# Two narrow projections made one unit: the low-rank gate and the forget gate of a hybrid decoder layer

## The reference

```
h = x + 0.5 * post1(swiglu1(pre1(x)))              # gate, up, down
p = preM(h) @ w_in                                 # 1024 -> 512 | 784 | 768 | 772 columns
ya = conformer_conv(p[A]); yb = gla(p[B]); yc = short_conv(p[C]); yd = fox(p[D])
h = h + postM(concat(ya, yb, yc, yd) @ w_out)
h = h + 0.5 * post2(swiglu2(pre2(h)))

gla:  q, k, v, g, a_lr = split(p[B])               # a_lr has 16 columns
      log_a = log_sigmoid(a_lr @ w_a2 + b_a) / 16  # decay of every state row, summed in chunks of 64
fox:  q, k, v = p[D][:768]; logf = log_sigmoid(p[D][768:] + b_f)   # 4 columns, one for a head
      scores = q k / 8 + cumsum(logf)[query] - cumsum(logf)[key]; softmax; @ v
      (sample positions: the same against 256 cached rows per sequence)
```

## Time and profile before

| | |
|---|---|
| median of 3 runs | 1095.44 us (1094.72 to 1095.91) |
| profiled execution, its own time | 1094.53 us |
| its span | 1092.7 us |
| mean granted TensorE clock | 0.993 of full |
| PE busy | 1064.1 us (97%), 8956 matmuls |
| DVE busy | 705.6 us (65%) |
| ACT busy | 550.6 us (50%) |
| POOL busy | 274.5 us (25%) |
| phase "in" of layer 0 | from about 211 to 325 us of the span; layer 1 from about 748 to 861 us |

### The profile page before, as it was taken

How to read it: one execution, slowest core, us unless ns; L and a number is a source line. 1 busy time by engine, 2 the same in 40 slices (tenths; PEclk the granted TensorE clock), 3 DMA queues, 4 the chain that set the end, 5 groups by cost and what they waited for, 6 DMA issues and landing times. The chain is left out here.

```text
span 1092.7 us, 24133 instructions
## 1 busy us (share of the span) xinstructions
PE 1064.1 (97%) x8956; PEld 1028.8 (94%) x8956; DVE 705.6 (65%) x1045; ACT 550.6 (50%) x887; POOL 274.5 (25%) x340
## 2 busy tenths in 40 slices
PE   6999999989999999999999999999899999999997
PEld 5999999988879999999999999998888899999997
DVE  5666644589995766654476665436999776666443
ACT  6544454554357644454474445446534675444542
POOL 3222221304504322220132223012053042222200
PEclk9999999999999999999999999999999999999999
DMA  7666677342726566656646666763426257656561
GB/s 269 207 186 180 179 222 232 98 155 79 232 78 196 155 193 180 184 166 187 188 127 203 180 180 188 232 186 117 139 79 209 79 190 217 180 179 176 178 181 53
DMA packets 63747, 186.92 MB, mean 171 GB/s; under 512 B 9515, under 2 KB 19763, under 8 KB 63539
## 3 DMA queue, kind: packets, MB, share of 16 engines
q1 hardware_dynamic: 63666, 185.81, 56.2%
HBM read 182.40 MB, written 3.38 MB: 170 GB/s over the span
## 5 line engine op out<-in xcount | busy, mean ns | idle before, releaser
L313 DVE TENSOR_TENSOR w_lo<-raw,w_hi 128x1024 fp32r<-128x1024 f32 (+1 forms) x316 | 411.1, 1306 | 332.0 <-ACT w_hi L303 331.8
L303 ACT ACTIVATE w_hi<-raw 128x1024 fp32r<-128x1024 f32 x336 | 342.9, 1026 | 283.0 <-PE ub L345 188.4
L343 PE MATMUL ub<-hg_hi,w_hi 128*128 128x264 f32 x960 | 278.7, 290 | 6.3 <-DVE proj L1315 6.3
L344 PE MATMUL ub<-hg_lo,w_hi 128*128 128x264 f32 x960 | 274.9, 286 | 0.0
L345 PE MATMUL ub<-hg_hi,w_lo 128*128 128x264 f32 x960 | 274.6, 286 | 0.0
L343 PE MATMUL ub<-act_hi,w_hi 128*128 128x264 f32 x704 | 200.5, 285 | 0.0
L345 PE MATMUL ub<-act_hi,w_lo 128*128 128x264 f32 x704 | 200.0, 284 | 0.0
L344 PE MATMUL ub<-act_lo,w_hi 128*128 128x264 f32 x704 | 199.1, 283 | 0.0
L343 PE MATMUL quad<-hg_hi,w_hi 128*128 128x264 f32 x688 | 196.4, 285 | 0.0
L344 PE MATMUL quad<-hg_lo,w_hi 128*128 128x264 f32 x688 | 194.9, 283 | 0.0
L345 PE MATMUL quad<-hg_hi,w_lo 128*128 128x264 f32 x688 | 194.8, 283 | 0.0
(11 more groups left out here) (252 smaller groups left out, 1314.4 us busy)
## 6 DMA issues: line engine op xcount, KB each, us to landing
raw<-in_w_gu SPq DMA_DIRECT2D x176, 512.0 KB, 4.1
raw<-in_w_dn SPq DMA_DIRECT2D x64, 512.0 KB, 4.1
raw<-in_w_in SPq DMA_DIRECT2D x44, 512.0 KB, 3.8
raw<-in_w_dn SPq DMA_DIRECT2D x32, 384.0 KB, 3.7
raw<-in_w_out SPq DMA_DIRECT2D x16, 512.0 KB, 3.7
pages<-in_cache_k SPq DMA_DIRECT2D x32, 128.0 KB, 3.3
pages<-in_cache_v SPq DMA_DIRECT2D x32, 128.0 KB, 3.1
con<-in_con SPq DMA_DIRECT2D x1, 1448.0 KB
```

The costliest lines, as they stand in the source:

```text
L303: eng.activation(w_hi[:, slot, 0:w], raw[:, slot, 0:w], ACT.Copy).then_inc(*sig("hi_ready", reps))
L313: eng.tensor_tensor(w_lo[:, slot, 0:w], raw[:, slot, 0:w], w_hi[:, slot, 0:w].bitcast(F32), ALU.subtract)\
L343: eng.matmul(out, a_hi, x_hi[:, k0 + k, :], start=(first and k == 0), stop=False)
L344: eng.matmul(out, a_hi, x_lo[:, k0 + k, :], start=False, stop=False)
```

## The change

The 16 columns of the low-rank gate and the 4 columns of the forget gate become one unit of 36 columns: columns 0 to 15 and 32 to 35, with zeros between. Phase "in" has 23 units then; the 24th place of the ring stays empty, so that later units keep their slots and the semaphore counts (the last unit counts twice). Every unit behind the first has a number one lower. `mix(l, n)` runs at step n-1 on ACT, DVE and SP, and behind unit n-1 on PE, so it stands at the same unit by content. Beyond that:

- PE's small matmul of the GLA gate goes from n=3 to n=4 (with the new numbers still behind unit 3); ACT's softplus of it and the scaling of q go from n=4 to n=3, so to step 2. DVE's part stays at n=4, so at step 3.
- The forget gate's softplus goes from n=2 to n=7 on ACT, its DVE chain from n=3 to n=9. It works on partitions 32 to 35 now.
- `decode_scores` goes from n=15 to n=14 on PE, ahead of the unit it stood behind, and ACT copies `qd` before `qm`.

The engines' instruction lists show three places. In them `w_hi` is the rounding of a unit, `h_sq<-mb` the start of the GLA gate's softplus, `ln_t` the forget gate's softplus and `z_t` and `y_sq` the DVE chains of the GLA gate and of the forget gate.

The diff, cut to its core:

```diff
-ALR, FG, BQ, BK, AG, BG, AV, BV, DQ, DKK, DVV, CC, CX, CB = 0, 1, 2, 3, 4, 6, 8, 10, 12, 14, 16, 18, 19, 22
-IN_WIDTH = [16, 4] + [P] * 22
+ALR, FG, BQ, BK, AG, BG, AV, BV, DQ, DKK, DVV, CC, CX, CB = 0, 0, 1, 2, 3, 5, 7, 9, 11, 13, 15, 17, 18, 21
+IN_UNITS = 23
+FG_ROWS = slice(32, 36)
+IN_WIDTH = [FG_ROWS.stop] + [P] * (IN_UNITS - 1)
...
-POOLED = tuple(range(14, 24))
+POOLED = tuple(range(13, 23))
...
+        def no_unit(phase, idx):
+            return phase == "in" and idx == IN_UNITS
+        def counted(phase, idx):
+            return 2 if phase == "in" and idx == IN_UNITS - 1 else 1
+        def empty_turns(layer, phase, slot):
+            if slot != IN_UNITS % RING:
+                return 0
+            return layer + (phase in ("out", "gu1", "dn1"))
...
             def mix(l, n):                                   # PE
-                if n == 3:
+                if n == 4:
                     after(l, proj=1)
                     pe.matmul(mb[2][:, 0:NT], par[0:16, ...], proj[0:16, ALR, :], ...).then_inc(*sig("b_z"))
...
-                if n == 15:
+                if n == 14:
                     decode_scores(l, 0)
                     decode_scores(l, 1)
+                if n == 15:
                     gla_outputs(l)
...
-                for n in range(GROUP, 24):
+                for n in range(GROUP, IN_UNITS):
...
-                    mix(l, n)
+                    mix(l, n + 1)
...
             def mix(l, n):                                   # ACT
-                if n == 4:
+                if n == 3:
                     after(l, b_z=1)
                     softplus(l, soft[:, :], mb[2][:, 0:NT], ...)
-                if n == 2:
-                    after(l, proj=2)
-                    softplus(l, lft[:, :], proj[0:H, FG, :], ...)
-                if n == 4:
-                    after(l, proj=3)
+                if n == 7:
+                    after(l, proj=1)
+                    softplus(l, lft[:, :], proj[FG_ROWS, FG, :], ...)
+                if n == 3:
+                    after(l, proj=2)
                     act.activation(proj[:, BQ, :], proj[:, BQ, :], ACT.Copy, scale=DK ** -0.5)
...
             def mix(l, n):                                   # DVE
-                if n == 3:
-                    after(l, d_sp=3, proj=2)
+                if n == 9:
+                    after(l, d_sp=3, proj=1)
                     log_sigmoid(l, lf[:, :], proj[FG_ROWS, FG, :], ..., "d_lf")
...
-                    mix(l, s)
+                    mix(l, s + 1)
```

More of the change, by code:

```diff
@@ L326, in fourth_unit @@
             first = PHASES[phase][0]
-            return dict(index=3, phase=phase, layer=l, width=COLS, slot=3, number=l * UNITS + first + 3, turn=l * (UNITS // RING) + first // RING)
+            return dict(index=3, phase=phase, layer=l, width=COLS, slot=3, number=l * UNITS + first + 3,
+                        turn=l * (UNITS // RING) + first // RING - empty_turns(l, phase, 3))
         def final(l, q):
@@ L335, in first_unit, with multiply_unit @@
             return dict(index=s, phase="gu0", layer=0, weights=ins["w_gu0"], row=s, width=COLS, slot=s, number=s, turn=0)
-        def multiply_unit(eng, out, slot, x_hi, x_lo, tiles, k0, first, last, reps, ready=None):
+        def multiply_unit(eng, out, slot, x_hi, x_lo, tiles, k0, first, last, reps, ready=None, count=1):
             for k in range(tiles):
@@ L622, in fox_scores @@
             def fox_scores(l, h):
-                after(l, d_qm=2, d_cf=2, proj=16, b_rs=2, b_og=3)
+                after(l, d_qm=2, d_cf=2, proj=15, b_rs=2, b_og=3)
                 for out, q0, n in ((fox_bank[h][:, 0:P], 0, P), (fox_bank[h][:, P:3 * P], P, TP)):
                     pe.matmul(out, qm[:, h, q0:q0 + P], proj[:, DKK + h // 2, 0:n], start=True, stop=False)
-                    mm = pe.matmul(out, const("sel", H * P, H)[:, h * P:(h + 1) * P], cf[:, 0:n], start=False, stop=True)
+                    mm = pe.matmul(out, sel[:, h * P:(h + 1) * P], cf[:, 0:n], start=False, stop=True)
                 mm.then_inc(*sig("d_sc"))
@@ L845, in rows, with softplus @@
                 return slice(CH * i, CH * (i + 1))
-            def softplus(l, out, x, bias, name):
+            def softplus(l, out, x, bias, one, name):
                 act.activation(out, x, ACT.Abs, bias=bias).then_inc(*sig(name))
@@ L852, in softplus @@
                 after(l, **{name: 2})
-                act.activation(out, out, ACT.Ln, bias=biases[0:out.shape[0], 2:3]).then_inc(*sig(name))
+                act.activation(out, out, ACT.Ln, bias=one).then_inc(*sig(name))
             def level_decays(l, i):
@@ L893, in mix @@
                 if n == 14:
-                    after(l, proj=14, d_qz=1)
-                    for i in range(2):
-                        act.activation(qm[rows(i), i::2, :], proj[rows(i), DQ:DQ + 2, :], ACT.Copy).then_inc(*sig("d_qm"))
+                    after(l, proj=13, d_qz=1)
                     for j in range(2):
@@ L902, in mix @@
                                .then_inc(*sig("d_qd"))
+                    for i in range(2):
+                        act.activation(qm[rows(i), i::2, :], proj[rows(i), DQ:DQ + 2, :], ACT.Copy).then_inc(*sig("d_qm"))
                 if n == 16:
@@ L1086, in level_keys @@
             def level_keys(l, i):
-                after(l, b_E=i, proj=4, b_qs=1)
+                after(l, b_E=i, proj=3, b_qs=1)
                 if i >= 3:
@@ L1148, in mix @@
                 if n == 12:
-                    after(l, proj=12)
+                    after(l, proj=11)
                     for j in range(2):
@@ L1178, in mix @@
                 if n == 16:
-                    after(l, proj=16)
+                    after(l, proj=15)
                     dve.wait_ge(zeroed, 1)
```

79 lines of the change are left out of this document (41 added, 38 removed).

## The result

The changed kernel is slower: 1101.79 us, the median of 15 runs (1096.04 to 1105.2), against 1095.16 (15 runs, 1093.02 to 1097.52). The ratio is 1.0061, 95% interval 1.0046 to 1.0077. I had forecast 1090.6 with 0.84 on faster. The difference is 0.6%, small but clear of the noise. The time of the changed kernel also spreads twice as wide as before.

What follows compares the result with a forecast made beforehand. At the first GLA levels the gate, softplus, running sum and decays chain was taken to bound, not PE. Gains of 2 x 2.43 = 4.9 us took the median from 1095.44 to 1090.6, own range 1089 to 1092.8, overall 1086.9 to 1094.0.

Steps and rivals of the forecast that it cites:

- The unit removed, the wider units, the first keys on DVE: Phase "in": 24 matmuls fewer a layer, wider units 0 and 1 cost PE nothing, DVE's first keys 2.68 us sooner.
- The first level after 1.6 us, for the evacuation of unit 2: First GLA level on PE: goes at 228.3 after about 1.6 us of waiting, needing unit 2's evacuation.
- the forecast waits: PE's waits ahead of the GLA levels: about 1.6 us before the first, about 2.2 us before the second.
- DVE's way to q, 34.0 us: DVE from first keys to q's evacuation: 34.46 becomes 34.0 us, the forget gate's chain filling waits for ACT.
- rival 3: Forget gate's softplus on ACT delays the decays and DVE keeps its waits: gain 0.2 us a layer, 1095 us; chance 0.09.
- The scores exposed, unit 16 at 276.1: PE waits 1 to 1.8 us for `qd`; unit 16 starts at 276.1, before 278.54: gain 2.4 us a layer.
- the gain is kept to the end of the layer: Behind unit 16: PE and DVE both start the unchanged stretch sooner, so unit 16's gain of 2.4 us lasts.
- meet no wait of PE: Moving the scores costs 1.8 us; values loaded sooner and less ACT waiting for DMA shorten no wait of PE.
- Rival 1: Unit 16 keeps full clock and ends 1.6 us sooner: 4.1 us a layer gained, 1087.3 us; chance 0.13.
- Rival 2: New or shifted PE waits bring more half clock from the scores on, 1.6 us a fall: 1097 us; chance 0.06.
- the range for all: Whole kernel: time range over the forecast and all rivals, 1086.9 to 1094.0 us.

Runs made afterwards that it cites:

- e2: Changed kernel with the input projection's fourth unit and the gate's product swapping banks, so the first level waits for three units, not four: 1095.90 us, ratio 1.0016.
- e1: Changed kernel with the output projection's third unit rounded sooner on ACT and its rest computed sooner on DVE: 1096.46 us, ratio 1.0008.
- e13: Changed kernel with POOL computing the rests of four late units for only 16 of 1024 columns: 1096.94 us, ratio 1.0028.
- e14: Kernel before the change, with POOL computing the rests of four late units for only 16 of 1024 columns: 1094.30 us, ratio 0.9995.
- e3: Changed kernel with the decode scores and the order of ACT's copies put back as before the change: 1098.93 us, ratio 1.0029.
- the two mends: The changes of e1 and e2, put together in the changed kernel: 1088.26 us, ratio 0.9947 to the kernel before.
- e8: Changed kernel with the two mends and four unread filler products ahead of each of the first two levels: 1085.82 us, ratio 0.9909.
- e10: Changed kernel with four unread filler products in PE's wait for the output projection's third unit: 1098.94 us, ratio 1.0036.

## Why the prediction was wrong, step by step

- **The unit removed, the wider units, the first keys on DVE.** Right: 24 matmuls a layer gone, unit 3 at its old place, the first keys 2.68 us sooner.
- **The first level after 1.6 us, for the evacuation of unit 2.** Wrong. It waited 3.95 us, for unit 3, because of the bank that the level shares with it. I had read which data the level needs and not which bank it writes. e2 gives the forecast waits and wins 4.2 us net.
- **DVE's way to q, 34.0 us, with the forget gate's chain for nothing.** Wrong. It took 35.85 (230.16 to 266.01). The waits for ACT were to be filled by the chain and were not: 2.0 us, 1.89 of them now at 238.47, behind the forget gate's softplus. That is the mechanism of rival 3, in the place that I had costed at nothing. But it comes of the step above: with the first level free (e2) the softplus has the cover that I had given it, DVE waits 0.2 us, and the way is 34.45.
- **The scores exposed, unit 16 at 276.1.** The stretch behind the scores was right (9.70 us, forecast 9.79), their start was not. Unit 16 started at 277.19; with the phase 0.69 us sooner that is a gain of 0.66 and not 2.43. The scores started 1.9 us later than forecast, which is DVE's way again (35.85 for 34.0). PE waited 0.55 us for them, not 1 to 1.8, because it was late itself. As a layer's sum up to the norm the gain was 2.2 and 0.9 us, the larger with unit 16 at full clock.
- **"Behind unit 16 order and content are as before ... the gain is kept to the end of the layer."** This is the step that turned the sign: 8.7 and 2.2 us were lost there. Order is not as before against the ring: the third output unit's round stayed at its step while the mixers moved on (3.8 us a layer, e1). And sooner is not harmless: what arrives sooner puts POOL's rests beside DVE's chain (about 3 us, e13 against e14).
- **The sooner transfers "meet no wait of PE".** Wrong by the same collision: e3, which undoes the sooner scores, is 2.9 us faster.
- **Rival 1, unit 16 at full clock.** It came in layer 0 and not in layer 1, and did not help. I had DVE just in time behind it; instead more of DVE's instructions fell beside POOL's. The wait of 2.95 us at the sums stands in the two layers with unit 16 at full clock (layer 0 after, layer 1 of e1). In the other 14 layers of the profiles with sooner scores, full rests on POOL and transfers not held, unit 16 fell, and the wait is 0.84 us or less. With POOL's work out (e13, layer 0) the full clock at unit 16 helps as rival 1 says, by 1.55 us to the sums.
- **Rival 2, slower by more falls of the clock (0.06).** This came, at 1101.8 instead of 1097, and at other places than I named: not behind the scores but behind the waits at the sums and the output. It deserved far more than 0.06: 5.3 of the 6.6 us are clock loss. And the range for all, up to 1094.0, left out rivals 2 and 3 (1097 and 1095), to which I had given 0.15.

What stays open: why the clock of one execution falls in unit 16 and that of another does not. The same kernel e1 took from 1088.9 to 1099.5 us, and only one execution of each kernel was profiled. The parts are not a clean sum either: the two mends together give more than each alone, through the clock.

## What to carry to other kernels

When units are renumbered in a ring, list what is placed by step and what by unit: what keeps its step is late against what moved. Before a wait is counted as shorter, read which bank its instruction writes, and with whose evacuation it shares it. A gain at the head of a phase is kept only where the engine that paces the rest has slack; DVE had none here, and what arrived sooner put its instructions beside POOL's.

## What the runs showed of the hardware

- Some instructions of DVE that start beside POOL's subtraction of 128 x 512 (1.3 us) end only behind it. Over all traces here the products of 64 x 16 (`pm`) ended 0.04 us behind POOL's end (17 times), the scaling of 256 values (`tail`) 0.15 (20 times), the products of 128 x 248 (`a_dec`) 0.27 (18 times). So the price is what is left of POOL's instruction: 0.16 to 1.05 us for one column, 0.40 to 1.42 for two of 64 x 16, 0.68 to 1.79 for a scan of 256. The taps, which read their running sum from PSUM (`quad`), were not held up: 760 of them started beside such a subtraction, and none took over 0.49 us (0.48 elsewhere). The Trainium skill (GPSIMD Engine Reference, 1. Specifications) says that POOL shares its SBUF interfaces with VectorE and contends with its instructions of two SBUF inputs, or in a 2-port mode. The rows agree for the products and the scan. The scaling has one tile as input besides one value a row; no run here shows in which mode it ran.
- Filler products that nobody reads, in a wait of 1.8 to 2 us, kept the granted clock at 1.00 where it was 0.50 to 0.60 behind the empty wait, in e8 (clock loss 10.2 to 5.8 us) and e10 (14.4 to 12.1). In e8 2.0 us of net were paid for them, in e10 nothing.
